# First modulation from four weight quarters in flight; the next layer's scale quarters beside the output tiles

## What is computed

```
def ada_params(cond_act, w, b):              # w: 1024 x 3072, one per layer
    mod = cond_act @ w + b
    return jnp.split(mod, 3, axis=-1)        # shift, scale, gate

act_lat, act_ctx = silu(c), silu(c_ctx)
for i in range(2):                           # 0: latent attention, 1: Fourier
    sh, sc, gt = ada_params(act_lat, w_ada[i], b_ada[i])
    u = rms_norm(h, norm_g[i]) * (1 + sc) + sh
    h = h + gt * mixer_i(u)                  # layer 0 also modulates the context, with act_ctx
```

## Time and profile before

| | us |
|---|---|
| median of 3 runs | 1455.04 |
| lowest and highest | 1453.71, 1455.94 |
| the profiled execution, its own time | 1455.69 |
| its span, first to last instruction | 1453.9 |
| TensorE busy in it | 1390.7 |
| VectorE busy in it | 750.4 |

### The profile page before, as it was taken

The page is one execution under the profiler, slowest core; times in us unless marked ns, Lnnn a source line. Parts: engine busy times, 40 slices in busy tenths (PEclk is TensorE's granted clock), DMA queues, the critical chain, the costliest instruction groups (busy, mean ns, idle before and its releaser), DMA issues.

```text
span 1453.9 us, 18237 instructions
## 1 busy us (share of the span) xinstructions
PE 1390.7 (96%) x6933; PEld 1150.4 (79%) x6933; DVE 750.4 (52%) x1024; ACT 578.7 (40%) x890; POOL 502.6 (35%) x235
## 2 busy tenths in 40 slices
PE   5799899999999999999999989999999999999998
PEld 2278787779988888877779879788888888888887
DVE  1389788853845437567443434450635435253342
ACT  4233455553533353545544434443334223232321
POOL 1133101126451394412324114124465444444441
PEclk9899999999999999989999889879999999999999
DMA  8676000117331142311223213113323333323331
GB/s 300 209 268 202 25 11 25 29 30 228 97 101 58 29 159 78 105 36 44 73 62 88 58 35 85 54 30 101 101 87 102 100 89 100 100 89 100 101 89 70
DMA packets 204501, 136.18 MB, mean 94 GB/s; under 512 B 7033, under 2 KB 185834, under 8 KB 204442
## 3 DMA queue, kind: packets, MB, share of 16 engines
q1 hardware_dynamic: 204442, 135.37, 30.9%
HBM read 130.64 MB, written 4.72 MB: 93 GB/s over the span
## 4 chain that ended last, share of the span: by engine, by line
PE 80%; DVE 10%; ACT 3%; DMA 2%; SPq 2%; issue 2%; POOL 1%; ACTq 0%; DVEq 0%; POOLq 0%
PE psum L1878 26%; PE psum L1879 25%; PE psum L1880 25%; DVE neg_max L1420 1%; DMA w_raw<-in_mla_w_in 1%; DVE pt_lo L1413 1%; PE psum L1919 1%; DVE probs L1408 1%; DMA w_raw<-in_fno_w_in 1%; POOL w_lo L610 1%; ACT probs L837 1%; PE psum L2275 1%; ACT w_hi L720 1%; PE psum L2042 0%; PE psum L2401 0%
## 5 line engine op out<-in xcount | busy, mean ns | idle before, releaser
L610 POOL TENSOR_TENSOR w_lo<-w_raw,w_hi 128x1024 fp32r<-128x1024 f32 x180 | 439.8, 2447 | 770.7 <-ACT w_hi L720 642.7
L1878 PE MATMUL psum<-u_hi,w_hi 128*128 128x512 f32 (+1 forms) x960 | 372.8, 388 | 6.8 <-DVE u_lo L1332 2.5
L1879 PE MATMUL psum<-u_lo,w_hi 128*128 128x512 f32 (+1 forms) x960 | 363.7, 379 | 0.0
L1880 PE MATMUL psum<-u_hi,w_lo 128*128 128x512 f32 (+1 forms) x960 | 363.4, 379 | 0.0
L720 ACT ACTIVATE w_hi<-w_raw 128x1024 fp32r<-128x1024 f32 x180 | 189.4, 1056 | 206.8 <-PE psum L1880 155.6
L1878 PEld LDWEIGHTS psum<-u_hi,w_hi 128*128 128x128 f32 x960 | 183.4, 191 | 46.2 <-issue 8.9
L1880 PEld LDWEIGHTS psum<-u_hi,w_lo 128*128 128x128 f32 x960 | 182.8, 190 | 34.1
L1879 PEld LDWEIGHTS psum<-u_lo,w_hi 128*128 128x128 f32 x960 | 183.4, 191 | 32.8 <-issue 1.7
L1878 PE MATMUL psum<-y_hi,w_hi 128*128 128x512 f32 x416 | 162.4, 390 | 0.0
L1879 PE MATMUL psum<-y_lo,w_hi 128*128 128x512 f32 x416 | 161.9, 389 | 0.0
L1880 PE MATMUL psum<-y_hi,w_lo 128*128 128x512 f32 x416 | 161.9, 389 | 0.0
(11 more groups left out here) (419 smaller groups left out, 2357.8 us busy)
## 6 DMA issues: line engine op xcount, KB each, us to landing
w_raw<-in_w_in SPq DMA_DIRECT2D x52, 512.0 KB, 3.8
w_raw<-in_w_up SPq DMA_DIRECT2D x32, 512.0 KB, 4.0
w_raw<-in_w_down SPq DMA_DIRECT2D x32, 512.0 KB, 3.6
ada_back<-in_w_ada SPq DMA_DIRECT2D x7, 2048.0 KB, 8.2
ada_w<-in_w_ada SPq DMA_DIRECT2D x5, 2048.0 KB, 9.6
w_raw<-in_fno_w_in SPq DMA_DIRECT2D x16, 512.0 KB, 3.8
w_raw<-in_mla_w_in SPq DMA_DIRECT2D x11, 512.0 KB, 9.0
w_raw<-in_mla_w_out SPq DMA_DIRECT2D x8, 512.0 KB, 3.7
```

Source lines behind the costliest of these rows:

```text
L610: pool.tensor_tensor(WL[:, j, :], RAW[:, j % 2, :], f(WH[:, j, :]), ALU.subtract).then_inc(lo_done, 1)
L1878: pe.matmul(out, ah, bh, start=first, stop=False)
L1879: pe.matmul(out, ah, bl, start=False, stop=False)
L1880: return pe.matmul(out, al, bh, start=False, stop=last)
```

## The change

- **Start of the loads.** SP issues the identity, x, quarter 0, the bias tables, then quarters 1, 2 and 3 without a wait: each has a buffer of its own (AQ; the third lies in u_lo's place, the fourth in that of the context's operands). Two tiles of A0, ctx and the rope tables follow. The fifteen small vector loads go to ScalarE's queue.
- **Start on TensorE.** Eighteen matmuls of ones by ones come first. x is transposed before and around the vectors, over 6 banks. The order is then ada(0), bias row, ada(1), turn of row 0, norm spread, ada(2), turn of row 1, one eighth of ada(3), turn of row 2, the rest of ada(3). The turn of row 3 comes inside the first layer product.
- **Start on ScalarE and VectorE.** x is copied out before its squares are summed. Shift and scale are formed in two halves, the first from quarters 0 and 2. A chunk is now one scalar_tensor_tensor out of the residual, the gain and the spread norm into PSUM, a high part on ScalarE, and one scalar_tensor_tensor for the low part. The eight separate normalizations (line 1294) fall away. The context's scaling moves from VectorE to ScalarE, ahead of the split of tile A0+2. A0's tiles 0 and 1 advance together, chunk by chunk, and the context is turned within tile 3.
- **Quarters 0 to 3 of modulation(r).** Their partial sums lie in PSUM up to the last of the eight instructions. Their loads and their column sums are placed anew: sums of 0 and 1 after gate tile 1, 2 after tile 3, 3 after tile 5.
- **Gate tile 7** moves behind first_units. **top()** becomes a single negated maximum, and MLA_SCALE goes into the gain mla_g_qa.
- **Quarters 4 and 5** (layer 1's scale) move out of G1 to the output tiles: their loads follow output tile 5 and the wait for the last head's output; VectorE multiplies them after the residual adds 0 and 1; TensorE sums them after output tile 3, ahead of the half tiles. Quarters 6 and 7 are loaded ahead of the Fourier layer's tiles, each after a wait for quarter 4's and 5's use.

The core of the diff:

```diff
-XN = at("x_normed", 104, [P, KC, T])
-AROW = at("ada_rows", 88, [2, 4, T])
+AROW = [at(f"ada_row{n}", 164 - 2 * n, [2, T]) for n in range(2)]
+AROW += [at("ada_row2", 166, [2, T]), at("ada_row3", 204, [2, T])]
...
+AQ = [AD[0], AD[1], at("ada_w2", 32, [P, KC, T]), AB[1]]
...
+    sp.dma_start(AQ[0][:], ada_weights(0)).then_inc(s_adaq[0], 16)
     sp.dma_start(T5[:], d["t5_bias_2"]).then_inc(s_t5, 16)
     sp.dma_start(HOT[:], d["bucket_hot"]).then_inc(s_t5, 16)
     sp.dma_start(MROW[:], d["mask_row"]).then_inc(s_t5, 16)
-    sp.dma_start(COS[:], d["rope_cos"]).then_inc(s_t5, 16)
-    sp.dma_start(SIN[:], d["rope_sin"]).then_inc(s_t5, 16)
-    sp.dma_start(HPICK[:], d["head_pick"]).then_inc(s_mask, 16)
+    for q in range(1, 4):
+        sp.dma_start(AQ[q][:], ada_weights(q)).then_inc(s_adaq[q], 16)
...
+    load_tile(A0, None, 2, d["mla_w_in"][:, 2 * P:3 * P], KC)
+    sp.wait_ge(ada_mm, 1)
+    gate_load(0)
+    key_rope_tile()
+    sp.wait_ge(row_ss, TT + 1)
+    sp.wait_ge(x_t, KC)
+    gate_load(1)
...
+    def gate_load(r):
+        sp.dma_start(ada_source(r)[:], ada_weights(4 + r)).then_inc(s_adaw[r % 2], 16)
...
+    sp.wait_ge(tile_done, 4)
+    gate_load(2)
+    gate_tile(4)
+    sp.wait_ge(ada_used, 2)
+    gate_load(3)
+    for r in range(5, 8):
+        gate_tile(r)
...
+    for j in range(6):
+        out_tile(j)
     sp.wait_ge(o_lo, HEADS)
-    for r in range(6, 8):
-        sp.dma_start(AB[r % 2][:], ada_weights(4 + r)).then_inc(s_adaw[r % 2], 16)
+    gate_load(4)
+    gate_load(5)
...
+    for r in range(6, 8):
+        sp.wait_ge(ada_used, r - 1)
+        gate_load(r)
...
+    act.wait_ge(row_ss, 9)
+    for m in range(TC // P):
+        act.activation(CTOK[:, m, :], CTOK[:, m, :], ACT.Copy, scale=RSC[:, TT + m:TT + m + 1]).then_inc(x_scaled, 1)
...
+    def lat_e(c):
+        if c >= 3:
+            v.wait_ge(u0_lo, c - 2)
+        v.scalar_tensor_tensor(u_stage(c), HT[:, c, :], MULL[0][:, c:c + 1], bank(3), ALU.mult, ALU.mult).then_inc(u0_e, 1)
+    def lat_lo(c):
+        v.wait_ge(u0_hi, c + 1)
+        v.scalar_tensor_tensor(UL[:, c, :], u_stage(c), ADAL[0][:, c:c + 1], f(UH[:, c, :]), ALU.add, ALU.subtract).then_inc(u0_lo, 1)
...
+        acc, w = ada_sum(r), ada_source(r)
+        part = acc if r >= 6 else bank(7 if r else 5)
+        link(v.tensor_scalar(part, w[:, 0, :], CACT[:, 0, 0:1], None, ALU.mult))
+        for k in range(1, KC - 1):
+            link(v.scalar_tensor_tensor(part, w[:, k, :], CACT[:, k, 0:1], part, ALU.mult, ALU.add))
+        v.scalar_tensor_tensor(acc, w[:, KC - 1, :], CACT[:, KC - 1, 0:1], part, ALU.mult, ALU.add).then_inc(ada_used, 1)
...
-        link(v.reduce_max(NMAX[:, 2 + par:3 + par], PB[:, (4 + 2 * par) * T:(4 + 2 * par) * T + TK], AX))
-        v.tensor_scalar(NMAX[:, par:par + 1], NMAX[:, 2 + par:3 + par], -MLA_SCALE, None, ALU.mult).then_inc(s_max, 1)
+        v.reduce_max(NMAX[:, par:par + 1], PB[:, (4 + 2 * par) * T:(4 + 2 * par) * T + TK], AX, negate=True).then_inc(s_max, 1)
...
     for c in range(4):
         v.wait_ge(tile_done, MO + c + 1)
         attention_added(c, bank(c), slice(0, T))
+        if c < 2:
+            modulation(4 + c)
+    v.wait_ge(ada_mm, ADA0 + 6)
+    link(v.tensor_tensor(ADAL[1][:, 8:16], mod[:, 16:24, 0], COLS[:, b0 + 32:b0 + 40], ALU.add))
+    link(v.scalar_tensor_tensor(MULL[1][:], ADAL[1][:, 8:16], 1.0, COLS[:, g0 + 8:g0 + 16], ALU.add, ALU.mult))
...
+    pe.wait_ge(ones_set, 1)
+    for _ in range(18):
+        pe.matmul(bank(6, P), ONES[:], ONES[:], start=True, stop=True)
...
     ada(0)
+    pe.wait_ge(bias_row, 1)
+    pe.wait_ge(x_copied, KC)
+    pe.matmul(bank(0), T5R[:], HOT[:, 0:T], start=True, stop=True)
+    pe.matmul(bank(1, P), T5R[:], HOT[:, T:TOEP], start=True, stop=True).then_inc(bias_mm, 1)
+    ada(1)
+    turn_row(0, 0)
     pe.wait_ge(diag_done, TT)
-    pe.wait_ge(x_copied, KC)
     for m in range(TT):
         mm = pe.matmul(bank(3, P, m * P), ONES[:], DIAG[:, m, :], start=True, stop=True)
     mm.then_inc(rs_mm, 1)
-    ada(1)
-    pe.wait_ge(bias_row, 1)
-    pe.matmul(bank(4), T5R[:], HOT[:, 0:T], start=True, stop=True)
-    pe.matmul(bank(5, P), T5R[:], HOT[:, T:TOEP], start=True, stop=True).then_inc(bias_mm, 1)
-    for q in range(2, 5):
-        ada(q)
+    ada(2)
+    turn_row(1, 1)
+    ada(3, 0, 1)
+    turn_row(2, 2).then_inc(ada_mm, 1)
+    ada(3, 1, KC)
...
+    pe.wait_ge(lo_done, 2)
+    pe.wait_ge(bias_row, 2)
+    for k in range(KC):
+        pe.wait_ge(u0_lo, k + 1)
+        for j in range(2):
+            mm = lat_step(j, k)
+            if k == KC - 1:
+                mm.then_inc(tile_done, 1)
+        if k == 0:
+            pe.wait_ge(mod_done, 1)
+            last_columns()
+    for j in range(2, 4):
...
-    for r in range(8):
+    for r in range(7):
+        if r < 2:
...
-        for x in {1: (0, 1), 2: (2,), 4: (3,), 6: (4,), 7: (5,)}.get(r, ()):
+        if r == 0:
+            lat_key_sums()
+        for x in {1: (0, 1), 3: (2,), 5: (3,)}.get(r, ()):
...
+    pe.wait_ge(lo_done, G1 + 8)
+    for k in range(KC):
+        mm = three(bank(3), wsl(WH, 3, k), wsl(WL, 3, k), UH[:, k, :], UL[:, k, :], k == 0, k == KC - 1)
+    mm.then_inc(tile_done, 1)
...
+    modulation(4)
+    modulation(5)
     for j in range(4):
...
```

More of the change, by code:

```diff
@@ L725, in _ @@
                 act.activation(CACT[:, :, n], COLS[:, 8 * n:8 * n + 8], ACT.Silu).then_inc(cact_done, 1)
+            for c in range(4, KC):
+                x_copy(c)
             act.wait_ge(s_x, 16)
@@ L756, in _ @@
             split_hi(A0, None, 3)
-            for q in range(1, 4):
-                ada_row_copy(q)
-            act.wait_ge(mod_done, 1)
-            for c in range(KC):
-                act.activation(UH[:, c, :], XN[:, c, :], ACT.Identity, scale=MULL[0][:, c:c + 1], bias=ADAL[0][:, c:c + 1]).then_inc(u0_hi, 1)
             for c in range(KC):
@@ L1311, in _ @@
[L1311 to L1332 removed]
+            v.wait_ge(bias_mm, 1)
@@ new lines, in _, with first_modulation @@
+            v.tensor_tensor(BROW[:], PB[:, 0:TOEP], MROW[:], ALU.add).then_inc(bias_row, 1)
+            b0, g0 = ROW["b_ada"], ROW["norm_g"]
+            def first_modulation(half):
+                chunks = slice(4 * half, 4 * half + 4)
+                two = lambda ap: ap.rearrange("p (g c) -> p g c", c=KC)[:, :, chunks]
+                part = bank(7, 32).rearrange("p (g c n) -> p g c n", g=2, n=2)[:, :, chunks, :]
+                bias = two(COLS[:, b0:b0 + 16])
+                v.tensor_tensor(two(ADAL[0][:, 0:16]), part[:, :, :, 0], bias, ALU.add)
+                link(v.tensor_tensor(two(ADAC[:]), part[:, :, :, 1], bias, ALU.add))
+                scales, weights = slice(KC + 4 * half, KC + 4 * half + 4), COLS[:, g0 + 4 * half:g0 + 4 * half + 4]
+                v.scalar_tensor_tensor(MULL[0][:, chunks], ADAL[0][:, scales], 1.0, weights, ALU.add, ALU.mult)
+                v.scalar_tensor_tensor(MULC[:, chunks], ADAC[:, scales], 1.0, weights, ALU.add, ALU.mult).then_inc(mod_done, 1)
+                v.wait_ge(mod_done, half + 1)
@@ L1333, in _, with ctx_chunks @@
+            def ctx_chunks():
+                ctx_e(0)
+                for c in range(KC):
+                    if c < KC - 1:
+                        ctx_e(c + 1)
+                    ctx_lo(c)
             swap = [16 + x for x in range(16)] + list(range(16))
@@ L1912, in ada @@
[L1912 to L1925 removed]
+            for c in range(5, KC):
+                turn_x(c)
@@ new lines, in ada, with turn_row @@
+            def ada(q, k0=0, k1=KC):
+                if k0 == 0:
+                    pe.wait_ge(s_adaq[q], 16)
+                for k in range(k0, k1):
+                    mm = pe.matmul(ada_row_bank(q)[0:2, :], CACT[:, k, :], AQ[q][:, k, :], start=k == 0, stop=k == KC - 1)
+                if k1 == KC:
+                    mm.then_inc(ada_mm, 1)
+            def turn_row(n, q):
+                pe.wait_ge(ada_row, n + 1)
+                for b in range(4):
+                    mm = pe.transpose(ada_columns(q)[:, 2 * b:2 * b + 2], AROW[n][:, b * P:(b + 1) * P], IDENT[0:2, 0:2])
+                return mm
```

290 lines of the change are left out of this document (140 added, 150 removed).

## The result

The changed kernel takes 1442.6 us (median of five runs, 1439.6 to 1446.3) for 1455.0: a ratio of 0.9913, 95% interval 0.9893 to 0.9932. Run again later beside other kernels it gave 0.9912 (0.9899 to 0.9924). So it is faster by 12 to 13 us where 18 were forecast: inside the range of 1427 to 1446, the right sign, and a third of the gain is missing. Its profiled execution is 13.1 us shorter than the one of before.

The account below looks back on a forecast made before the run. TensorE's work and its few idle stretches bound the kernel; 18.5 - 0.7 - 0.9 + 7.0 + 4.0 - 10.0 = 17.9 us less than the profiled 1455.69, 1437.8; as median 1437, range 1427 to 1446.

Parts of the forecast that it names:

- rival (c): Start gives 6 us less through ScalarE's longer list or TensorE's low clock: 1443 us, chance 0.13.
- The start: Up to the first layer product: at 46.8 for 65.3, 18.5 us gained, less 0.7 for a possible low clock.
- (d): Start: the four quarters land together, ada(0) 21 us later than forecast; 1458 us, slower, chance 0.03.
- A0: A0's tiles: a new 2.4 us wait for tile A0+2, plus clock and squares; 0.9 us lost.
- G1 and units: Gate tiles and first units: two quarter sums leave, gate tile 7 covers the wait before first scores; 7.0 us gained.
- top(): Attention: 32 multiplications go, 25 of them on the path; 4.0 us gained, bounds 1 and 6.
- Output tiles: Half tiles queue behind both sums of quarters 4 and 5, start 8.6 us later, plus low clock: 10.0 us lost.
- (a): Output tiles lose only 6 us and top() gives its 6: 1431 us, chance 0.14.
- (b): Output tiles: VectorE's quarters stretched to 10 us each in place of 6, 8 more: 1445 us, chance 0.12.
- The rest: The kernel's remaining later stages: shift whole, with a forecast difference of 0 us.
- Rival (e): Gain given back because a later stage is bound by its own loads: within 0.2% of before, chance 0.03.

Follow-up runs that it names:

- negated_max_only: Kernel before with only the row maximum negated in the same VectorE instruction and the scale folded into the query's gain: 1452.1 us, ratio 0.9974.
- two_loads: Changed kernel with two of the four quarters in flight at the start, quarters 2 and 3 issued after earlier row products: 1444.3 us, ratio 0.9923.
- gate_in_g1: Changed kernel with the last gate tile back at the end of the gate tiles, ahead of the first head's units: 1447.6 us, ratio 0.9948.
- late_sums: Changed kernel with quarters 4 and 5 formed behind residual adds 2 and 3 and summed inside the fourth half tile: 1432.7 us, ratio 0.9852.
- two_step_top: Changed kernel with the maximum and its negation as two VectorE instructions again, the scale still folded into the gain: 1444.3 us, ratio 0.9940.
- sum_in_sbuf: Changed kernel with the running sum of scale quarters 0 to 5 in SBUF in place of a PSUM bank: 1447.0 us, ratio 0.9953.

## Why the prediction was right or wrong

The median, 1442.6, lies beside rival (c)'s 1443, but the start did not give less; what is missing was lost at three other places. By the table the start and A0 came out 2.0 us better than forecast and the other rows 6.8 worse, so the difference of 4.8 us hides errors that cancel. In the prediction's working two figures do not fit its rows: 4.4 for 3.6 in A0 is 0.8, not 0.9, and the attention's clock of 0.98 is below 1.00 too; it is the low clock under the first scores that the G1 term counts.

**The start** (18.5 less 0.7) came nearly as worked out: first product at 46.91 for 46.8, row products of 7.03 each, no low clock. Quarter 0 came 0.7 late (15.6 for 14.9) and the work from there on took 0.6 less than summed (31.3 for 31.9), which cancel by luck. The kernel before itself is known no better than that: negated_max_only, with the same start, had its first product at 64.10 for 65.28. The reason was half right. That the row products are the bound and not the number of loads in flight is what two_loads shows. Of the vectors' move the prediction said that it frees the queue and gave it no price: it is 3.0 us of the 18.4. The matmuls of ones were rightly given nothing. Rivals (c) and (d) fall: the quarters landed one after another, and each but the first was there when asked for.

**A0.** The wait was forecast at 2.4 us and measured 2.05, at the place named; the squares' 0.6 was 0.79. The 1.4 of low clock behind it did not come in this profile, but 1.5 did in six of the ten profiles of kernels with this wait. 0.5 gained for 0.9 lost, and that the low clock stayed away is luck.

**G1 and units.** 6.4 for 7.0. gate_in_g1 bears out the whole cover.

**top().** 2.6 for 4.0. The step that failed is the count of those on the path. 25 of 32 lay on the chain of work that ended last, and each was given its 0.17 in full. TensorE gained 0.08 for each: it stands behind VectorE at fewer places than there were multiplications (17 for 23 in the window), and at ten of those its wait shrank by 0.06 on average, for a reason that no run isolates. The 8.0 us of waits that the prediction leaned on the earlier trace rows hold 3.58 and 1.77 at the first two heads, outside that window. The chain tells who was last, not by how much.

**Output tiles.** This is the term that was most mis-sized: 12.9 lost for 10.0. Sign and mechanism were right (half tiles queued behind both sums). Of the 11.1 us gap for 8.6: quarter 4 landed 10.3 us after its issue, and VectorE began at 308.8 for 307.5 (335.4 less the 27.9 by which this stretch had moved by then); its quarters then took 0.3 more, since the first instruction of each took 0.75 for 0.5; and the second sum ran at the low clock, 0.9 more. The low clock behind the gap cost 2.7 for 1.4, since it lasted 5.9 us of the half tiles, and 0.9 came back, mostly where TensorE had waited 0.74 for the norm. Rivals (a) and (b) fall: the loss was not 6, and each quarter took 6.2 us, not 10. The Trainium skill ("SBUF — State Buffer", section "SBUF: two separate sides") has VectorE and GpSimd exclude each other when VectorE reads two SBUF inputs. The 36 accumulating instructions with a PSUM input, at 754 to 758 ns (six of them ran across GpSimd's split at 317.7), and up to 2775 ns once the sum lay in SBUF, agree with it.

**What it left out.** The prediction priced this loss and took it as given. It did not ask whether TensorE needs the sums there at all. late_sums answers that: no. The step at fault is the place that the change gave the two sums, not VectorE's time.

**The rest** did not shift whole but grew by 1.9 us. 1.5 of that lie behind 405.10, inside the 2.6 us over which that work varies between kernels. Rival (e), the whole gain given back, falls.

## What to carry to other kernels

When work is moved to a place where an engine is idle, look at what consumes its result and put the consumer as late as its own user allows: two small sums ahead of independent matmuls cost 9 us that a new order of the same instructions gave back. Price a removed instruction by the waits of the bounding engine that it can shorten, and not by its own duration times its count on the chain: here half of that was worth nothing. And a wait before TensorE has two prices, itself and the clock: 3.6 us of idle cost 1.6 more, two waits of 8.3 us together cost 3.6 more, and about 2 us (2.6 in one) cost nothing in four profiles and 1.5 in six.

## What the hardware showed that was not expected

- The low clock outlasts a gap. After 8.25 us of idle time within 11.1, the second sum and the half tiles ran at the lower of TensorE's two levels (granted clock 0.5: 1.2 for 2.4 GHz) from 322.0 to about 329.5. After 1.91 us of idle time at 13.7 there was none, after 3.57 at 13.4 there was. After the wait in A0 (2.05 us, at the same place in the same work) there was none in four profiles, both of the changed kernel among them, and 1.5 us of it in five (two_step_top: granted clock 0.53 from 60.4 to 64.0), so the length of the gap alone does not tell.
- VectorE's plain multiplication of 128 x 512 took 0.75 us from SBUF into PSUM where it takes 0.48 to 0.49 from SBUF into SBUF (sum_in_sbuf); the accumulating one takes 0.75 into either, when no split on GpSimd runs beside it.
- One of VectorE's smallest instructions, forming the first half of the scale (128 x 4) from two SBUF tensors, took 2.08 us at 41.19, beside a split on GpSimd from 40.91 to 43.25, and 0.16 at 49.22 with no split beside it. The first chunk was still ready in time, at 46.1 for 46.9.
- Two 2 MB loads that are issued when the way is nearly free landed 7.6 and 8.0 us after their issue; the same load behind 0.5 MB landed in 10.3.
